# Layer 0's modulation rows over four column groups of TensorE, turned by a selector product

## The chip, the cores and the metric

One core of one Trainium2 chip runs the whole program. The metric is the device time of one execution in microseconds (us). The engines are TensorE (PE in the profile), VectorE (DVE), ScalarE (ACT), GpSimd (POOL) and SyncE (SP, which here only issues transfers). Each runs its own instruction list in order and they meet only at semaphores.

## The reference, cut to what matters

Two transformer blocks of two layers each run over 512 tokens of width 1024 (the first block carries 256 context tokens as well, 768 in all). At the head of each layer stands a modulation: a small matrix product of two conditioning vectors with a large weight.

```python
mod   = silu(c)     @ w_mod[l] + b_mod[l]     # for the 512 tokens
mod_c = silu(c_ctx) @ w_mod[l] + b_mod[l]     # for the 256 context tokens
sh1, sc1, ga1, sh2, sc2, ga2 = split(mod, 6)  # 1024 values each
h = rmsnorm(x, g_norm1[l]) * (1 + sc1) + sh1
pf, ... = split_proj(h @ w_in[l])             # pf: 256 Fourier features
y_f = fourier_mix(pf)
x = x + ga1 * (concat(y_f, y_m, y_a) @ w_out[l])
```

The change concerns layer 0 alone, and of it the first three of the six parts: shift (sh1), scale (sc1) and gate (ga1), 3072 values for each of two vectors. Everything is float32. Large products are made from values split in a high and a low part; the modulation's are plain float32 products.

## The kernel before

**Modulation tiles.** The weight of these 3072 columns comes as 12 tiles of 1 MB (`modw[0..11]`; 128 partitions, `KC` = 8 slices of 256 columns). They go through four slots (`MOD_FIRST`, each 2048 arena columns). `mod_row` (L799) works one tile: 8 products, each with a stationary operand of two columns (the two conditioning vectors' slice k, `cact`) and a moving operand of 256 columns, summed over k in PSUM on partitions 0 and 1. The profile shows two MATMUL records for each plain float32 product, so a tile is 16 records. Tiles 0 to 3 (shift) fill pair 0, tiles 4 to 7 (scale) pair 1, tiles 8 to 11 (gate) pair 2. A "pair" is two PSUM banks, 1024 columns.

**Turning.** ACT copies a pair's two rows to SBUF (`mod_rows`, L1588, into `rows_first`), and `turn(g)` (L807) makes eight PE transposes of 2 x 128 to bring the values onto partitions (into pair 3). DVE adds the bias there (`bias_added`).

**Order on PE.** `first_mod`: tiles 0 to 3, tiles 4 and 5, `turn(0)`, tiles 6 and 7. `norm`: column sums of squares for the rmsnorm (L780, L822), then `turn(1)`. `norm_mod` (L826): tiles 8 to 11. Then `fourier(768)`: `first_jobs` (L717), two feature jobs over 8 chunks k, 96 products in all, each chunk behind `h_wait(k)`, the signal that DVE has made `h_lo` chunk k. Then `pair_read(0)` and `pair_read(1)`, which wait until ACT has copied both jobs' results to `f_pf`; `turn(2)`; six jobs of the channel transform (L780), whose results DVE copies out in `values_read` (L2462); then the token transform (L929, L932) and the output projection (L712).

**Order on SP.** Conditioning vectors, tiles 0 to 3, x (3 MB), tiles 4 to 7, weight tile w0 into `raw[0]`, tiles 8 to 11, weight tile w1 into `raw[1]`, then `late_mod(12)` into `raw[0]` (a modulation tile that DVE folds, once w0 is split), `late_mod(13)` into `raw[1]` once w1 is split, and on. Each tile after the fourth waits until PE is done with the tile that last had its slot (`mod_used`).

**Order on ACT.** `mod_rows(0)`, eight squares of x, `mod_rows(1)`, the high part of w0 (`split`, L1551), the root of the norm (L1664, L1665), eight high parts of h (L1670), `mod_rows(2)`, the load of the Fourier constants, and in `fourier`: first the high part of w1 (`split`), then the two `f_pf` copies (L1741).

**Order on DVE.** The conditioning's silu, sums of squares, the low part of w0 (L2268), bias and gain, the chunks of h (L2483, L2490), and in `fourier`: the low part of w1, `late_fold(12)` (four long reductions, L2352), the gate's bias (after `turn(2)`), `values_read`, `late_fold(13)`.

Of the kernel before, what the change touches and what calls it, by code (L numbers as in the profile page):

```python
# [16 lines left out]
P = 128  # L17
# [85 lines left out]
def program(nc, io, per_pass):  # L103
    with ExitStack() as ctx:
# [3 lines left out]
        def sem(name):  # L108
            return ctx.enter_context(nc.semaphore(name))
# [114 lines left out]
        mod_folded = sem("mod_folded")  # L224
        rows_in = sem("mod_rows_in_sbuf")
        rows_turned = sem("mod_rows_turned")
        max_scores = sem("max_scores_ready")
        max_done = sem("max_reduced")
        maxt = sem("max_transposed")
# [18 lines left out]
        mod_first = [area(8 * T_ALL + i * KC * 256, KC, 256) for i in range(MOD_FIRST)]  # L248
        mod_ring = [area(12 * T_ALL + i * 2 * D, 2, D) for i in range(MOD_RING)]
        fold_products = area(4 * T_ALL, 2, D)  # L250
        rows_first = area(8 * T_ALL + MOD_FIRST * KC * 256, 1024, parts=2)

        n_sq = [area(i * T_ALL, T_ALL) for i in range(2)]
        n_acc = area(2 * T_ALL, T_ALL)
# [239 lines left out]
        def _(sp):  # L494
            t = Tally(sp, "sp", per_pass)
            def mod_tile(ti, slot):
                sp.dma_start(mod_first[slot].rearrange("p a b -> p (a b)"), io["modw"][ti]).then_inc(mod_in[slot], 16)

            sp.dma_start(small[:, 0:64], io["cv"]).then_inc(cv_in, 16)
            def mod_tiles(first, end):  # L500
                for ti in range(first, end):
                    if ti >= MOD_FIRST:

                        sp.wait_ge(mod_used, ti + 1)
                    mod_tile(ti, ti % MOD_FIRST)
            n_tiles = io["wt"].shape[0]

            def first_weights(*tiles):
# [20 lines left out]

            mod_tiles(0, MOD_FIRST)  # L530
            sp.dma_start(x[:].rearrange("p a b -> p (a b)"), io["xt"]).then_inc(x_in, 16)
            mod_tiles(MOD_FIRST, MOD_EARLY)
            first_weights(0)
            mod_tiles(MOD_EARLY, MOD_ROWS)
            first_weights(1)

            sp.wait_ge(w_lo_done, 0 + 3)
# [133 lines left out]
        def _(pe):  # L671
# [42 lines left out]
                                           stop=(k == kc - 1 and i == 2))  # L714
                mm.then_inc(signal, 1)

            def first_jobs(w, outs, n, signals):  # L717

                for k in range(KC):
                    h_wait(k)  # L720
                    for c, out in enumerate(outs):
                        for i, (a, b) in enumerate(passes(w, H)):
                            for lo, hi in segments(n):
                                mm = pe.matmul(out[:, lo:hi], a[:, k * 256 + c * P:k * 256 + (c + 1) * P], b[:, k, lo:hi],  # L724
                                               start=(k == 0 and i == 0), stop=(k == KC - 1 and i == 2))
                        if k == KC - 1:
                            mm.then_inc(signals[c], 1)
# [58 lines left out]
            def first_mod():  # L786

                pe.wait_ge(dve_pe, t.next(dve_pe))

                for ti in range(MOD_EARLY):  # L790
                    if ti % 4 == 0:
                        take_pair(ti // 4)
                    if ti == 6:

                        pe.wait_ge(const_in["start"], 32)
                        turn(0)
                    mod_row(ti, pp[ti // 4][0:2, ti % 4 * 256:(ti % 4 + 1) * 256])

            def mod_row(ti, out):  # L799

                slot = ti % MOD_FIRST
                pe.wait_ge(mod_in[slot], t.next(mod_in[slot], 16))
                for k in range(KC):
                    mm = pe.matmul(out, cact[:, 0, :, k], mod_first[slot][:, k, :], start=(k == 0), stop=(k == KC - 1))  # L804
                mm.then_inc(mod_used, 1)

            def turn(g):  # L807

                pe.wait_ge(rows_in, t.next(rows_in))
                for c in range(8):  # L810
                    at = S + 16 * g + 2 * c
                    mm = pe.transpose(pp[3][:, at:at + 2], rows_first[:, c * P:(c + 1) * P], ident[0:2, 0:2])
                mm.then_inc(rows_turned, 1)

            def norm(n):
# [7 lines left out]
                mm.then_inc(job_act, 1)  # L823
                turn(1)

            def norm_mod():  # L826

                take_pair(2)
                for ti in range(MOD_EARLY, MOD_ROWS):
                    mod_row(ti, pp[2][0:2, ti % 4 * 256:(ti % 4 + 1) * 256])  # L830

            def h_wait(k):

                pe.wait_ge(h_ready, t.next(h_ready))
# [67 lines left out]
            def fourier(n):  # L902
                w = tile()
                take_pair(0)
                take_pair(1)
                if n == S:
                    raw_first_jobs(w, (pp[0], pp[1]), S, False, tail_places(T_ALL), 2, (job_dve, tile_used))
                    t.next(h_ready, KC)
                else:
                    first_jobs(w, (pp[0], pp[1]), n, (job_act, tile_used))  # L910
                pair_read(0)
                pair_read(1)

                if n > S:
                    turn(2)
                pe.wait_ge(const_in["fourier"], t.next("fourier", 16))
                nt = n // P
                for i in range(nt):
                    tok = slice(i * P, (i + 1) * P)
                    plain_job(i % 2, [(pp[i % 2][:, c * 256:(c + 1) * 256], f_pf[:, c, tok], f_b, True, True)  # L920
                                      for c in range(2)], job_dve)
                pair_read(0)
                pair_read(1)
                for c in range(2):
                    cols = [slice(c * 256 + a * P, c * 256 + (a + 1) * P) for a in range(2)]
                    take_pair(c)
                    for a in range(2):
                        for i in range(NT):
                            mm = pe.matmul(pp[c][:, a * S:a * S + SH], f_v[:, i, cols[a]], f_c[:, a, i, :], start=(i == 0),  # L929
                                           stop=(i == NT - 1 and n == S), skip_group_check=True)  # L930
                        for i in range(2 if n > S else 0):
                            mm = pe.matmul(pp[c][:, a * S + SH:a * S + SH + CH], f_v[:, NT + i, cols[a]], f_cc[:, a, i, :],  # L932
                                           start=False, stop=(i == 1), skip_group_check=True)
                    mm.then_inc(job_act, 1)
                out_proj(2, P, n, 1, 8, 1024, fourier_wait)
# [568 lines left out]
            barrier()  # L1504
            first_mod()
            norm(T_ALL)
            norm_mod()
            for layer in range(2):
                n = T_ALL if layer == 0 else S
                fourier(n)  # L1510
# [14 lines left out]
        def _(act):  # L1525
# [48 lines left out]
            def first_mod():  # L1574
                act.dma_start(prm[:], io["prm"][0]).then_inc(const_in["prm"], 16)
                act.wait_ge(cv_in, 16)
                act.activation(cact[:], cvec, ACT.Exp, scale=-1.0).then_inc(act_dve, 1)

                act.wait_ge(cact_done, 1)
                for at in (0, 2):  # L1580
                    act.dma_start(io["crow"][at:at + 2].rearrange("v (p k) -> p v k", k=KC), cact[:, at])\
                       .then_inc(crow_out, 16)
                mod_rows(0, 0)
                for j in range(KC):
                    square(j, T_ALL)
                mod_rows(1, 1)

            def mod_rows(g, p):  # L1588

                act.wait_ge(mod_used, MOD_FIRST + 4 * (g + 1))  # L1590
                if g:
                    act.wait_ge(rows_turned, g)
                finish(act.activation(rows_first, pp[p][0:2, :], ACT.Copy), pair_free[p], rows_in)

            def spread_conditioning(slot, row):
                act.dma_start(crow[:, slot, :], io["crow"][row:row + 1].to_broadcast([P, D])).then_inc(crow_in, 16)

            def late_rows():
                mod_rows(2, 2)
                fourier_constants()  # L1600

            def square(j, n):

# [132 lines left out]
            def fourier(n):  # L1736
                if n > S:
                    split()
                for c in range(2 if n > S else 0):
                    job(last=c == 1)  # L1740
                    act.activation(f_pf[:, c, 0:n], pp[c][:, 0:n], ACT.Copy).then_inc(pair_free[c], 1)  # L1741
                k = SH + CH if n > S else SH
                for c in range(2):
                    job()
                    act.activation(f_s[:, c, 0:k], pp[c][:, S:S + k], ACT.Copy).then_inc(act_dve, 1)

                    act.wait_ge(dve_act, t.next(dve_act))
                    act.activation(u_hi[:, c, 0:n], f_y[:, c, 0:n], ACT.Copy).then_inc(act_dve, 1)
                split()
# [458 lines left out]
            act.dma_start(gfin[:], io["gfin"]).then_inc(const_in["start"], 16)  # L2208
            barrier()
            first_mod()  # L2210
            split()
            norm(T_ALL, 0)
            late_rows()
            for layer in range(2):
                n = T_ALL if layer == 0 else S
                if layer:
# [19 lines left out]
        def _(dve):  # L2236
# [143 lines left out]
            def first_mod():  # L2380
                heard()
                finish(dve.tensor_scalar(cact[:], cact[:], 1.0, None, ALU.add))
                finish(dve.reciprocal(cact[:], cact[:]))
                finish(dve.tensor_tensor(cact[:], cact[:], cvec, ALU.mult), dve_pe, cact_done)

                dve.wait_ge(x_in, 16)
                dve.sem_inc(x_done, KC)
                for j in range(KC):
                    add_square(j, T_ALL)
                for s in range(MOD_RING):  # L2390
                    t.next(mod_in[s], 16 * (MOD_ROWS // MOD_FIRST))
                split()

                dve.wait_ge(const_in["prm"], t.next("prm", 16))
# [1039 lines left out]
```

## Time and profile before

| | us |
|---|---|
| median of 3 runs | 3429.74 |
| lowest, highest | 3429.38, 3435.35 |
| profiled execution, first to last instruction | 3431.3 |
| PE busy in it | 3316.9 (97%) |
| from the start to the first product of the token transform (L929) | 82.20 |

The page gives one execution; its span is 1.6 us above the median of the timed runs. PE is busy in nearly all of it. The stage that the change touches is the first 82 us. A timeline row gives its start and length in us, the engine, the line, the operation, the output and inputs, and the number of instructions merged; in brackets stands the idle time before it and what ended it. SPq and ACTq rows are transfers being issued, not the transfers themselves.

### The profile page before, as it was taken

The numbers are of one execution on the slowest core, as the hardware profiler recorded it, in microseconds if no ns is written. First come the engines' busy times: TensorE is split into PE (matmuls) and PEld (weight loads), VectorE is DVE, ScalarE is ACT, GpSimd is POOL, SyncE is SP. The second block draws the span as 40 slices with busy tenths as digits, with TensorE's granted clock in tenths as the row PEclk, the third lists the DMA queues.
The fourth block names the chain that finished last, engine by engine and source line by source line (L and its number), as shares of the span: only waits on it lengthen the run. The fifth ranks groups of instructions, "written<-read, shape, count | busy, mean of one in ns | idle before, by whom it ended". The sixth has DMA issues, their size and how long they took to land.

```text
span 3431.3 us, 42870 instructions
## 1 busy us (share of the span) xinstructions
PE 3316.9 (97%) x16496; PEld 2652.5 (77%) x16496; DVE 2051.2 (60%) x2561; ACT 1248.9 (36%) x1564; POOL 337.2 (10%) x328
## 2 busy tenths in 40 slices
PE   8999989999999998999998999999999999999999
PEld 4777768888887776688885677788887577878887
DVE  4676777555466566565567755465557766364443
ACT  3245353221223454532234533242225433343222
POOL 0000011100111000111121100011112011001000
PEclk9999999999999999999999999999999999999999
DMA  6331123323222222154432122244443132222223
GB/s 277 112 108 59 60 81 123 112 98 130 102 98 76 78 79 79 42 198 171 171 133 70 54 68 84 98 150 178 165 168 107 36 99 71 92 102 92 93 97 110
DMA packets 61594, 370.59 MB, mean 108 GB/s; under 512 B 9416, under 2 KB 10056, under 8 KB 20368
## 3 DMA queue, kind: packets, MB, share of 16 engines
q1 hardware_dynamic: 45120, 275.31, 22.9%
q10 hardware_dynamic: 16336, 93.39, 7.3%
q8 instruction: 93, 1.52, 0.2%
q14 instruction: 45, 0.37, 0.0%
HBM read 354.27 MB, written 2.33 MB: 104 GB/s over the span
## 4 chain that ended last, share of the span: by engine, by line
PE 80%; DVE 12%; ACT 5%; issue 3%; DMA 1%; POOL 0%; DVEq 0%; ACTq 0%; SPq 0%; POOLq 0%
PE pair L712 50%; PE pair L1185 8%; PE pair L863 6%; PE pair L750 2%; PE pair L780 2%; DVE w_lo L2268 2%; PE pair L1018 1%; PE pair L1254 1%; PE pair L724 1%; ACT w_hi L1551 1%; PE pair L804 1%; PE pair L1080 1%; DVE mxg L2862 1%; PE pair L1237 1%; PE pair L1388 1%
## 5 line engine op out<-in xcount | busy, mean ns | idle before, releaser
L2268 DVE TENSOR_TENSOR w_lo<-raw,w_hi 128x2048 fp32r<-128x2048 f32 x221 | 509.8, 2307 | 284.1 <-ACT w_hi L1551 279.1
L1551 ACT ACTIVATE w_hi<-raw 128x2048 fp32r<-128x2048 f32 x221 | 421.6, 1908 | 619.6 <-PE pair L712 523.2
L712 PE MATMUL pair<-h_hi,w_hi 128*128 128x512 f32 (+2 forms) x1856 | 595.5, 363 | 5.7 <-DVEq L2250 2.7
L712 PE MATMUL pair<-h_lo,w_hi 128*128 128x512 f32 (+2 forms) x1856 | 594.5, 362 | 0.0
L712 PE MATMUL pair<-h_hi,w_lo 128*128 128x512 f32 (+2 forms) x1856 | 594.3, 362 | 0.0
L712 PE MATMUL pair<-u_hi,w_hi 128*128 128x512 f32 x1116 | 373.3, 370 | 12.2 <-DVEq L2260 4.9
L712 PE MATMUL pair<-u_hi,w_lo 128*128 128x512 f32 x1116 | 370.8, 367 | 0.0
L712 PE MATMUL pair<-u_lo,w_hi 128*128 128x512 f32 x1116 | 370.7, 367 | 0.0
L2531 DVE TENSOR_TENSOR u_lo<-arena,u_hi 128x512 fp32r<-128x512 f32 (+1 forms) x128 | 97.2, 759 | 447.3 <-POOL arena L3099 447.0
L712 PEld LDWEIGHTS pair<-h_hi,w_hi 128*128 128x128 f32 (+2 forms) x1856 | 309.4, 183 | 67.7 <-issue 7.3
L712 PEld LDWEIGHTS pair<-h_hi,w_lo 128*128 128x128 f32 (+2 forms) x1856 | 309.5, 183 | 61.2
L712 PEld LDWEIGHTS pair<-h_lo,w_hi 128*128 128x128 f32 (+2 forms) x1856 | 309.4, 183 | 60.4
L2309 DVE SCALAR_TENSOR_TENSOR x<-pair,mod,x 128x512 f32<-128x512 f32 x336 | 223.5, 690 | 162.4 <-PE pair L712 148.8
L3099 POOL TENSOR_TENSOR arena<-arena 128x512 f32<-128x512 f32 (+1 forms) x128 | 172.1, 1345 | 1339.5 <-ACT u_hi L1702 1247.2
L1701 ACT ACTIVATE arena<-pair 128x512 f32<-128x512 f32 (+1 forms) x120 | 78.2, 652 | 462.9 <-PE pair L712 462.8
L712 PEld LDWEIGHTS pair<-u_hi,w_hi 128*128 128x128 f32 x1116 | 193.9, 189 | 50.9 <-issue 7.6
L1185 PE MATMUL pair<-h_hi,w_hi 128*128 128x512 f32 x544 | 226.8, 417 | 1.8 <-DVE w_lo L2268 1.5
L2365 DVE CUSTOM_DVE_ANT_0 arena<-arena,crow 128x1024 f32<-128x1024 f32 x192 | 225.1, 1219 | 0.0
L712 PEld LDWEIGHTS pair<-u_lo,w_hi 128*128 128x128 f32 x1116 | 194.0, 189 | 34.8 <-issue 0.2
L712 PEld LDWEIGHTS pair<-u_hi,w_lo 128*128 128x128 f32 x1116 | 193.6, 189 | 35.0
L1185 PE MATMUL pair<-h_lo,w_hi 128*128 128x512 f32 x544 | 215.9, 397 | 0.0
L1185 PE MATMUL pair<-h_hi,w_lo 128*128 128x512 f32 x544 | 215.3, 396 | 0.0
(377 smaller groups left out, 4888.6 us busy)
## 6 DMA issues: line engine op xcount, KB each, us to landing
raw<-in_wt_dram SPq DMA_DIRECT2D x222, 1024.0 KB, 4.8
arena<-in_modw_dram ACTq DMA_DIRECT2D x72, 1024.0 KB, 5.0
arena<-in_modw_dram SPq DMA_DIRECT2D x12, 1024.0 KB, 8.7
raw<-in_modw_dram SPq DMA_DIRECT2D x12, 1024.0 KB, 4.7
arena<-arena SPq DMA_DIRECT2D x136, 64.0 KB, 2.0
arena<-negm_rows_dram ACTq DMA_DIRECT2D x16, 384.0 KB, 4.3
x<-in_xt_dram SPq DMA_DIRECT2D x1, 3072.0 KB, 18.6
arena<-in_fconst_dram ACTq DMA_DIRECT2D x2, 1414.0 KB, 6.1
```

Source lines behind the costliest of these rows:

```text
L712: mm = pe.matmul(pp[p][0:m, lo:hi], a[0:rows, k * width + c0:k * width + c0 + m], b[0:rows, k, lo:hi], start=(k == 0 and i == 0), stop=(k ...
L750: mm = pe.matmul(out[:, lo:hi], a[:, k * 256 + c * P:k * 256 + (c + 1) * P], v, start=first, stop=(k == KC - 1 and i == 2 and (not spread ...
L780: mm = pe.matmul(out, a, b, start=first, stop=last)
L863: mm = pe.matmul(pp[c + 1][:, lo:hi], a[:, k * 512 + c * P:k * 512 + (c + 1) * P], b[:, k, lo:hi], start=(k == 0 and i == 0), stop=(k == 3 ...
L1185: mm = pe.matmul(bank(slot), a[:, k * width + c0:k * width + c0 + P], b[:, k, 0:S], start=(k == 0 and i == 0), stop=(k == KC - 1 and i == 2))
L1551: act.activation(w_hi[slot][:], raw[slot][:], ACT.Copy).then_inc(w_hi_done, 1)
L1701: finish(act.activation(m_r[c][:, 0:n], pp[p][:, 0:n], ACT.Relu), pair_free[p])
L2268: dve.tensor_tensor(w_lo[slot][:], raw[slot][:], w_hi[slot][:].bitcast(F32), ALU.subtract)\
L2309: ins = dve.scalar_tensor_tensor(x[:, j, a:b], pp[p][:, a:b], mod[:, 16 + 24 * which + j, s:s + 1], x[:, j, a:b], ALU.mult, ALU.add)
L2365: ins = dve.tensor_tensor_reduce(out=w if v == vectors - 1 else fold_products[:, a, :], in0=w, in1=crow[:, v, :], scale=1.0, scalar=0.0, o ...
L2531: dve.tensor_tensor(u_lo[:, 2 * half + c, 0:n], m_f[c][:, 0:n], U32[:, 2 * half + c, 0:n], ALU.subtract).then_inc(hid_lo, 1)
L3099: pool.tensor_tensor(m_f[i % 2][:, 0:n], m_r[i % 2][:, 0:n], m_r[i % 2][:, 0:n], ALU.mult)\
```

## The change

Each modulation product now writes 32 partitions. The stationary operand is 32 columns wide (`cond_rows`: 16 copies of each of the two vectors), and slices k = 2g and 2g + 1 go to output partitions 32g to 32g + 31, in two rounds over g = 0 to 3. So a pair holds four partial sums, of two slices each. `cond_rows` lies in `raw[1]`, the place of weight tile w1. ACT copies all 128 partitions instead of two. `turn` makes eight plain float32 products of a 128 x 128 stationary slice of `rows_first` with a moving operand of two columns, `row_sel`, which has a one at partitions 32g (or 32g + 16) and adds the four partial sums while it turns them.

The four gate tiles leave `norm_mod`: two are worked before chunk 5 of `first_jobs`, two after its end. All four use slots 2 and 3. w0 is loaded ahead of tiles 6 and 7; w1 is loaded only after PE is done with tile 11. ACT splits w0 before `mod_rows(1)`, issues the load of the Fourier constants right after `mod_rows(1)`, and does `mod_rows(2)` after the `f_pf` copies.

```diff
@@ SP
-                        sp.wait_ge(mod_used, ti + 1)
-                    mod_tile(ti, ti % MOD_FIRST)
+                        sp.wait_ge(mod_used, ti + 1 if ti < MOD_EARLY else ti + 3)
+                    mod_tile(ti, mod_slot(ti))
...
-            mod_tiles(MOD_FIRST, MOD_EARLY)
+            mod_tiles(MOD_FIRST, 6)
             first_weights(0)
+            mod_tiles(6, MOD_EARLY)
             mod_tiles(MOD_EARLY, MOD_ROWS)
+
+            sp.wait_ge(mod_used, MOD_FIRST + MOD_ROWS)
             first_weights(1)
@@ PE
+                    if k == 5 and between:
+                        between()
                     h_wait(k)
...
-                for k in range(KC):
-                    mm = pe.matmul(out, cact[:, 0, :, k], mod_first[slot][:, k, :], start=(k == 0), stop=(k == KC - 1))
+                for half in range(2):
+                    for g in range(4):
+                        k = 2 * g + half
+                        mm = pe.matmul(out[32 * g:32 * g + 32], cond_rows[:, k, :],
+                                       mod_first[slot][:, k, :], start=(half == 0), stop=(half == 1))
...
-                    mm = pe.transpose(pp[3][:, at:at + 2], rows_first[:, c * P:(c + 1) * P], ident[0:2, 0:2])
+                    mm = pe.matmul(pp[3][:, at:at + 2], rows_first[:, c * P:(c + 1) * P], row_sel, start=True, stop=True)
...
-                    first_jobs(w, (pp[0], pp[1]), n, (job_act, tile_used))
+                    first_jobs(w, (pp[0], pp[1]), n, (job_act, tile_used), lambda: gate_mod(MOD_EARLY))
+                    gate_mod(MOD_EARLY + 2)
...
-            norm_mod()
@@ ACT
+                split()
                 mod_rows(1, 1)
+                fourier_constants()
...
-                finish(act.activation(rows_first, pp[p][0:2, :], ACT.Copy), pair_free[p], rows_in)
+                finish(act.activation(rows_first, pp[p][:], ACT.Copy), pair_free[p], rows_in)
...
+                if n > S:
+                    mod_rows(2, 2)
...
-            split()
             norm(T_ALL, 0)
-            late_rows()
@@ DVE
-                finish(dve.tensor_tensor(cact[:], cact[:], cvec, ALU.mult), dve_pe, cact_done)
+                finish(dve.tensor_tensor(cact[:], cact[:], cvec, ALU.mult), cact_done)
+                finish(dve.tensor_copy(cond_rows.rearrange("p k (v r) -> p k v r", r=16),
+                                       cact[:, 0].rearrange("p v k -> p k v").unsqueeze(3).to_broadcast([P, KC, 2, 16])),
+                       dve_pe)
+
+                dve.wait_ge(const_in["start"], 32)
+                finish(dve.tensor_reduce(row_sel, ident[:].rearrange("p (j w) -> p w j", w=32)[:, 0:32:16, :], AX.X, ALU.add),
+                       sel_ready)
```

## Rows read from the trace of the kernel before

**Rows 1.** The page: span, and busy time of each engine.

```profile
span 3431.3 us, 42870 instructions
...
PE 3316.9 (97%) x16496; PEld 2652.5 (77%) x16496; DVE 2051.2 (60%) x2561; ACT 1248.9 (36%) x1564; POOL 337.2 (10%) x328
```

**Rows 2.** Chain of waits, first 135 us: start, length, what.

```profile
13.50 11.27 DMA arena<-in_modw_dram
...
42.91 13.91 PE pair L804 x64
56.82 17.15 PE pair L724 x96
...
75.54 5.84 PE pair L780 x24
...
81.41 0.70 DVE arena L2462
```

**Rows 3.** Timeline of SP's issues, first 50 us.

```profile
28.55 11.36 SPq L497 DMA_DIRECT2D arena<-in_modw_dram  x4
39.96 0.43 SPq L512 DMA_DIRECT2D raw<-in_wt_dram  x1
```

**Rows 4.** Stretches: busy us by engine, then granted clock, DMA share, GB/s.

```profile
25.00:28.50 3.50, 3.50 (x17) 1.35 (x16) 2.17 (x3) 3.07 (x4) 0.00 (x0) 1.00 1.01 426
```

**Rows 5.** Timelines from 7 and from 42 us: the modulation products.

```profile
7.15 6.10 PE L804 MATMUL pair<-arena,cact 128*2 128x256 f32 x15 [7.15 <-DMA arena<-in_modw_dram]
...
42.84 13.98 PE L804 MATMUL pair<-arena,cact 128*2 128x256 f32 x64
```

**Rows 6.** Timeline of PE: grouped-query scores, two 64-row halves of the array.

```profile
1844.21 0.39 PE L1224 MATMUL pair<-u_hi 64*128 64x512 f32 x2
1844.44 0.39 PE L1224 MATMUL pair<-u_hi,u_lo 64*128 64x512 f32 x2
```

**Rows 7.** Timeline of PE: products with four and two moving columns.

```profile
3080.13 0.25 PE L733 MATMUL pair<-shift,w_hi 128*128 128x4 f32 x1
3080.24 0.25 PE L735 MATMUL pair<-shift,w_lo 128*128 128x2 f32 x1
```

**Rows 8.** Timeline, 42 to 48 us: turning, the norm's root, first chunks.

```profile
42.26 0.65 PE L812 MATMUL pair<-ident,arena 2*128 2x2 f32 x8
...
43.67 0.84 ACT L1665 ACTIVATE arena<-arena 128x768 f32<-128x768 f32 x1
...
45.00 0.18 DVE L2403 TENSOR_TENSOR mod<-pair,prm 128x32 f32<-128x32 f32 x1
...
45.43 2.21 DVE L2483 SCALAR_TENSOR_TENSOR arena<-x,gain,arena 128x512 f32<-128x512 f32 x4
...
47.77 1.15 DVE L2490 SCALAR_TENSOR_TENSOR h_lo<-arena,mod,h_hi 128x512 fp32r<-128x512 f32 x2
```

**Rows 9.** Stretches around an idle TensorE; columns as in Rows 4.

```profile
90.80:93.10 2.30, 0.38 (x4) 0.18 (x2) 1.15 (x4) 0.51 (x2) 0.00 (x0) 1.00 0.02 7
...
94.90:97.90 3.00, 2.93 (x9) 2.54 (x10) 2.16 (x2) 0.83 (x1) 0.00 (x0) 0.50 0.00 0
```

**Rows 10.** Timeline, 61 to 83 us, ACT and DVE: what follows w1's arrival.

```profile
61.63 1.00 ACT L1593 ACTIVATE arena<-pair 2x1024 f32<-2x1024 f32 x1
...
63.25 1.92 ACT L1551 ACTIVATE w_hi<-raw 128x2048 fp32r<-128x2048 f32 x1 [0.62 <-ACT arena L1593]
65.20 2.29 DVE L2268 TENSOR_TENSOR w_lo<-raw,w_hi 128x2048 fp32r<-128x2048 f32 x1 [2.30 <-ACT w_hi L1551]
...
72.11 0.08 DVE L2352 DVE_READ_ACCUMULATOR2_ANT mod_sum<- 128x1 f32 x1
...
74.01 0.81 ACT L1741 ACTIVATE arena<-pair 128x768 f32<-128x768 f32 x1 [0.25 <-PE pair L724]
...
76.71 1.48 DVE L2462 COPY arena<-pair 128x512 f32<-128x512 f32 x2 [0.96 <-PE pair L780]
```

**Rows 11.** Transfers issued from 60 to 80 us: size, median us to landing.

```profile
raw<-in_wt_dram SPq DMA_DIRECT2D x1, 1024.0 KB, 4.7
```

More of the change, by code:

```diff
@@ L226, in program @@
         rows_turned = sem("mod_rows_turned")
+        sel_ready = sem("row_selector_ready")
         max_scores = sem("max_scores_ready")
@@ L250, in program, with mod_slot @@
         fold_products = area(4 * T_ALL, 2, D)
-        rows_first = area(8 * T_ALL + MOD_FIRST * KC * 256, 1024, parts=2)
+        rows_first = area(8 * T_ALL + MOD_FIRST * KC * 256, 1024)
+        row_sel = small[:, 74:76]
+        cond_rows = raw[1][:, 0:KC * 32].rearrange("p (k w) -> p k w", w=32)
+        def mod_slot(ti):
+            return ti % MOD_FIRST if ti < MOD_EARLY else 2 + ti % 2
         n_sq = [area(i * T_ALL, T_ALL) for i in range(2)]
@@ L715, in feature_job, with first_jobs @@
                 mm.then_inc(signal, 1)
-            def first_jobs(w, outs, n, signals):
+            def first_jobs(w, outs, n, signals, between=None):
                 for k in range(KC):
+                    if k == 5 and between:
+                        between()
                     h_wait(k)
@@ L793, in first_mod @@
                     if ti == 6:
-                        pe.wait_ge(const_in["start"], 32)
+                        pe.wait_ge(sel_ready, 1)
                         turn(0)
-                    mod_row(ti, pp[ti // 4][0:2, ti % 4 * 256:(ti % 4 + 1) * 256])
+                    mod_row(ti, pp[ti // 4][:, ti % 4 * 256:(ti % 4 + 1) * 256])
             def mod_row(ti, out):
-                slot = ti % MOD_FIRST
+                slot = mod_slot(ti)
                 pe.wait_ge(mod_in[slot], t.next(mod_in[slot], 16))
-                for k in range(KC):
-                    mm = pe.matmul(out, cact[:, 0, :, k], mod_first[slot][:, k, :], start=(k == 0), stop=(k == KC - 1))
+                for half in range(2):
[3 more added lines that the diff above has]
+                                       mod_first[slot][:, k, :], start=(half == 0), stop=(half == 1))
                 mm.then_inc(mod_used, 1)
@@ L824, in norm, with gate_mod @@
                 turn(1)
[L826 to L830, printed above, removed]
+            def gate_mod(first):
+                if first == MOD_EARLY:
+                    take_pair(2)
+                for ti in range(first, first + 2):
+                    mod_row(ti, pp[2][:, ti % 4 * 256:(ti % 4 + 1) * 256])
             def h_wait(k):
@@ L1592, in mod_rows @@
                     act.wait_ge(rows_turned, g)
-                finish(act.activation(rows_first, pp[p][0:2, :], ACT.Copy), pair_free[p], rows_in)
+                finish(act.activation(rows_first, pp[p][:], ACT.Copy), pair_free[p], rows_in)
             def spread_conditioning(slot, row):
                 act.dma_start(crow[:, slot, :], io["crow"][row:row + 1].to_broadcast([P, D])).then_inc(crow_in, 16)
-            def late_rows():
-                mod_rows(2, 2)
-                fourier_constants()
             def square(j, n):
@@ L2390, in first_mod @@
                 for s in range(MOD_RING):
-                    t.next(mod_in[s], 16 * (MOD_ROWS // MOD_FIRST))
+                    t.next(mod_in[s], 16 * sum(mod_slot(ti) == s for ti in range(MOD_ROWS)))
                 split()
```

## The prediction

> **What bounds the kernel now.** I read the page first: PE is busy 3317 of 3431 us [rows 1]. What delays PE anywhere shifts all behind it, as each engine works its list in order and no later stretch is slack for PE, so the question is when PE reaches a point behind the change. I take the start of the token transform (L929), 82.20 before.
>
> Then the chain of waits [rows 2]. Tile 4 of the modulation arrives at 24.77, and PE is the chain nearly throughout from there: tiles 4 to 7 and the norm until 42.91, the four gate tiles (13.91 us), the 96 products of the Fourier jobs (17.15 us), six channel jobs (5.84 us), a last copy. Behind the chain stands memory: between 25 and 28.5 us the transfers fill their engines at 426 GB/s [rows 4], so 1 MB lands every 2.46 us. SP's list [rows 3] shows when PE is done with slots: the last issue of the four starts 0.43 us before 39.91, at 39.5, and that is the end of tile 7.
>
> **Tiles 4 to 7.** A tile is 16 records of 0.218 us (13.98 / 64), 3.5 us; the first ones, from 7.15, came 0.41 us apart (6.10 / 15), the half level of the clock, though the granted clock is written as full there [rows 5]. How fast the new products go no row shows. Bounds: no overlap, 3.5 us a tile; full overlap of four groups, 0.87 us. The nearest rows are the attention scores over two row halves of the array: a pair of products with 512 columns starts every 0.23 us [rows 6], while one product over the full array averages 0.24 us for 512 columns (96 products of 512 or 256 columns in 17.15 us [rows 2]). So independent parts of the array do work at the same time when neighbours in the list use different ones. In the new list the neighbours are different groups only every other time: a float32 product is two records, and both use the same group. If PE starts products in order, the second record of group 0 waits for the first, group 1's first starts with it, and so on: eight steps of 0.218 us, 1.75 us a tile. I take that.
>
> The Trainium skill ("TensorE: Matmul & The Clock Gate", Part 3) says that packed products start about 4 ns apart, which would make a tile 0.87 us; it also says that products start and end in program order, from which the halving follows. No row here has column groups. The skill's "TensorEngine Tiling (Array Packing)", Tiling Modes, adds that a change of mode drains the engine; with some twelve changes that speaks against the change, by an amount that no row shows.
>
> The order of landing becomes tile 4 at 24.8, tile 5 27.2, w0 29.7, tile 6 32.2, tile 7 34.6, since w0 goes ahead of two tiles. PE now waits for memory: tile 7 ends at 34.6 + 0.1 + 1.75 = 36.5, against 39.5. Of the 7 us that the products of four tiles save, 4 go to the wait for memory.
>
> **Norm and turn(1).** From 39.5 to 42.91 is 3.4 us, of which the eight transposes are 0.65 [rows 8], so the norm is 2.8. The turn becomes 16 records, each with 128 stationary columns. Products with four and two moving columns start 0.11 us apart [rows 7], so 1.8 us (bounds 0.65, were they as cheap as transposes, and 3.6 at the half clock). Turn(1) ends at 36.5 + 2.8 + 1.8 = 41.1. The norm's root ended at 44.51, 5.0 after tile 7 [rows 8], now 41.5. Before, DVE began the bias only at 45.00, after the low part of w0; that is now earlier and gone from the path. First chunk product: 41.1 + 0.1 + 0.43 = 41.6, against 45.43. The first chunk of h is done 3.5 us later (48.92 before), at 45.1.
>
> **The Fourier jobs.** Before, PE began them at 56.82, with the gate tiles as cover for DVE's chunks. Now it begins at 45.1 after 4 us of idleness. After a stretch with 0.38 of 2.3 us busy, the granted clock was 0.50 for 3 us [rows 9]. I add 1.7 us, half of some 3.4. Chunks come every 2.1 us (DVE: two products and two low parts of 0.55 and 0.57 us each [rows 8]), PE needs 17.15 / 8 = 2.1, so PE doesn't catch up. The gate tiles add 4 x 1.75 = 7.0. Tiles 10 and 11 are loaded when 8 and 9 are done, some 8 us before PE wants them. PE is done with tile 11 at X = 45.1 + 17.15 + 1.7 + 7.0 = 71.0, against 73.97 for the jobs before. So far a gain of 3.0.
>
> **w1, the step that decides.** Before, w1 was asked for at 39.96 [rows 3] and split at 63.25, beside PE's jobs. `cond_rows` now lies in `raw[1]`, so SP asks for w1 only at X. Queued behind that wait are late tiles 12 and 13 and w2. And ACT's list has the split of w1 ahead of the two `f_pf` copies, for which PE waits in `pair_read`. From X:
> - w1 lands at +4.7 [rows 11], ACT starts at +4.85 and ends at +6.8 (1.92 [rows 10]).
> - ACT: copies 2 x 0.81, `mod_rows(2)` 1.0, to +9.5. PE: turn(2) to +11.3, then two channel jobs to +13.3; it needs a pair back for the third.
> - DVE: low part of w1 to +9.1 (2.29). Tile 12, asked for right behind w1, landed at +7.3. Fold to +13.8 (from 67.5 to 72.2 before, 4.7 [rows 10]), hidden then behind the jobs and exposed now, since the fold stands ahead of `values_read` in DVE's list. Bias, first copy: +14.8 (0.69).
> - Four channel jobs of 0.97, last copy 0.7, reactions 0.2: L929 at +19.6. PE idled 9.5 us before, so its clock is low again; much of that hides behind DVE, and I add 0.8 (bounds 0 and 4).
>
> L929 starts at 71.0 + 20.4 = 91.4, 9.2 us later than 82.20. Behind it the lists are as before: fold 13 follows `values_read`, w2 is asked for at +13.8 and needed over 10 us later. So the 9.2 us stay.
>
> **What is free.** DVE's copy into `cond_rows` and the sum for `row_sel`: DVE has nothing else before x lands, and PE waits for tile 0 until 7.15 [rows 5]; were tile 0 earlier, some 0.4 us. ACT's copy of 128 partitions in place of two: same columns, 1.0 us. The constants and two spreads are issued by ACT while PE does the norm. Were they 0.6 us slower, they would delay the root.
>
> **Rivals.**
> A, the forecast: two-fold overlap and w1's load on the path, +9.2, 62%. Own range +8 to +15 (half clock in tiles 6 and 7, the norm, the turns and the channel jobs).
> B, full overlap: each tile 0.87 us. Tile 7 ends 0.9 earlier, the gate tiles save 3.5 more; X = 66.6, L929 87.0, +4.8, 3434.5 us. That is not slower as far as can be told. For it: rows 6, where a pair costs as one. Against: the two records of one group stand next to each other. It decides from the point where a tile falls under some 1.2 us, as the loss is then under 6.9. 22%. (The page on TensorE of the Trainium skill, Part 3, states this case's mechanism.)
> C, no overlap: a tile stays at 3.5. Tile 7 ends at 24.9 + 14.0 + 1.8 (turn) + 1.7 (clock) = 42.4, X = 83.8, L929 104.2, +22, 3451.8. For it: wide float32 operands were never seen in parallel here. 12%.
> D, faster: w1's split is hidden after all (it would have to be off ACT's list before the copies, which the code denies), with full overlap and a clock that stays up. Then the channel jobs start at X + 1.1 + 1.8, that is 66.6 + 2.9 - 1.7 = 67.8, against 75.54: -7.7, 3422.0. With the two-fold overlap and a falling clock it is only -1.6. 4%. That the change doesn't do what it says (groups not used at all) is C.
>
> **How the numbers follow.** The sum is made against the profiled execution, 3431.3 + 9.2 = 3440.5; the timed median is 1.6 lower, so 3438.9. 0.2% is 6.9 us, about what a measurement of this kernel can tell from no change. The range takes in B less 1 us and A with every clock penalty: 3433.5 to 3446; C and D, 16%, stay out. Slower: A nearly whole and C, 72%. Same: B and the low edge of A, 24%. Faster: D, 4%.
>
> **What would show it.** A tile's eight products in 1.75 us at full clock, tile 7 done by 36.5 and h's first chunk at 45; the start of w1's transfer at the end of tile 11, ACT waiting for it and PE idle for 9 us; fold 12 ahead of the first copy of `values_read`; L929 at 91. Wrong would make it: a tile of 0.9 or 3.5 us; a copy of `f_pf` ahead of w1's split; a stretch behind L929 that takes up the delay.

## The result

| | before | changed |
|---|---|---|
| timed runs, median | 3431.39 us (12 runs) | 3439.33 us (12 runs) |
| ratio to before | 1 | 1.0019 (95% interval 1.0012 to 1.0026) |
| end of tile 7 | 39.5 | 37.1 |
| first Fourier jobs start | 56.8 | 46.0 |
| all modulation tiles and first jobs done | 74.0 | 69.4 |
| token transform starts | 82.2 | 90.3 |

The change makes the kernel slower, by 1.9 in a thousand, 6.5 us (4.1 to 8.9); the two medians lie 7.9 us apart. The forecast was 9.2 us at the start of the token transform; there the profile shows 8.1 (90.27 against 82.20).

The chain of waits of the changed kernel, first 140 us (start, length, what), goes through the decisive stretch. The line numbers have moved: L817 is the modulation products (L804 before), L735 the first jobs (L724), L791 the channel jobs (L780), L826 the turns, L945 the token transform (L929).

```profile
16.92 18.22 DMA arena<-in_modw_dram
35.15 0.04 issue
35.19 1.93 PE pair L817 x16
...
45.99 13.04 PE pair L735 x60
59.03 1.86 PE pair L817 x32
60.90 6.56 PE pair L735 x36
67.45 1.91 PE pair L817 x32
69.36 0.02 issue
69.38 4.70 DMA raw<-in_wt_dram
...
75.91 1.49 ACT arena L1754 x2
77.41 0.92 ACT arena L1610
...
78.58 3.55 PE pair L826 x16
82.13 7.33 PE pair L791 x24
89.46 0.02 issue
89.48 0.70 DVE arena L2482
...
90.27 1.98 PE pair L945 x8
```

Where [rows 2] had PE nearly alone from 42.91 on, two transfers stand in the chain now. The first is the wait for tile 7, which lands at 35.15. The second begins when PE is done with tile 11, at 69.36: w1 is asked for at 69.38 and lands 4.70 later. Two rows of the timeline show what stood behind it on ACT, where [rows 10] had the split at 63.25 beside PE's jobs.

```profile
74.10 1.91 ACT L1566 ACTIVATE w_hi<-raw 128x2048 fp32r<-128x2048 f32 x1 [15.45 <-DMA raw<-in_wt_dram]
...
75.91 1.49 ACT L1754 ACTIVATE arena<-pair 128x768 f32<-128x768 f32 x2
```

ACT sat idle 15.45 us for w1, and the two `f_pf` copies came only after its split, at 75.91, although the jobs had ended at 67.45. DVE had a chain of its own behind w1: its low part and then fold 12, whose last row stands here with the first copy of `values_read`:

```profile
82.95 0.08 DVE L2365 DVE_READ_ACCUMULATOR2_ANT mod_sum<- 128x1 f32 x1
...
84.15 0.69 DVE L2482 COPY arena<-pair 128x512 f32<-128x512 f32 x1 [0.79 <-PE pair L791]
```

DVE waited 0.79 us for PE's first channel job, so in this kernel the chain over ACT and PE ended last, by that little. PE stood still from 69.4 to 78.6, and its clock had fallen when it went on. The stretches show that (busy us of PE, PEld, DVE, ACT and POOL, each with its instructions, then granted clock, DMA share, GB/s; cf. [rows 9]):

```profile
44.00:51.00 7.00, 5.01 (x15) 4.30 (x16) 6.87 (x14) 3.97 (x8) 0.00 (x0) 0.53 0.62 217
51.00:59.00 8.00, 8.00 (x50) 6.85 (x50) 7.87 (x16) 4.50 (x8) 0.00 (x0) 0.99 0.01 2
69.50:78.40 8.90, 0.00 (x0) 0.00 (x0) 2.36 (x2) 4.22 (x4) 0.00 (x0) 0.62 0.60 236
78.60:85.50 6.90, 6.90 (x25) 6.25 (x26) 5.26 (x10) 0.00 (x0) 0.00 (x0) 0.51 0.63 209
```

The turn and the first two channel jobs ran at the half level (0.51), and so did the first chunks of the jobs after the idle time before them (0.53).

The span of this one profiled execution is 3431.0 us, no longer than the 3431.3 of before. The 8 us had not gone at first: the low part of one weight tile starts at 1318.71 against 1311.21, still 7.5 late. Some 5 us of it were made up around 1900, where in the profiled execution of before the clock was low once more and in this one it was not. From the start of one low part on DVE to the start of another, the same 324 products took 74.42 us before and 69.29 us in the changed kernel:

```profile
1848.08:1922.50 74.42, 68.85 (x324) 40.21 (x322) 56.17 (x65) 34.45 (x48) 1.28 (x1) 0.91 0.12 40
```

```profile
1855.82:1925.11 69.29, 63.11 (x324) 37.22 (x322) 56.07 (x65) 34.38 (x48) 1.28 (x1) 1.00 0.13 43
```

Whether that is chance I can't say. The same stretch took 69.3 to 70.1 us in the profiles of all five kernels that work the gate tiles among and after the first jobs (changed, rows elsewhere, copies first, moves alone, a group's slices in a row), 74.5 in that of late w1 in the kernel of before, and 71.5 to 74.5 in those of the other four.

Single executions of one kernel lie some 10 us apart (3427.8 to 3435.8 us before, 3432.2 to 3443.7 after), so I judge a stage by the start of the token transform in its profile, and a version by the ratio of its timed runs.

### The profile page after: what moved, and what is told of

The parts are those of the page before. It is cut to its first block, busy times and chain, and to the rows that moved or that the text cites. A ratio compares the mean times of both kernels' runs of the same rounds, so it can differ in the third digit from the quotient of the medians.

```text
span 3431.0 us, 42940 instructions
## 1 busy us (share of the span) xinstructions
PE 3294.4 (96%) x16520; PEld 2648.4 (77%) x16520; DVE 2050.4 (60%) x2563; ACT 1249.1 (36%) x1564; POOL 340.8 (10%) x328
## 4 chain that ended last, share of the span: by engine, by line
PE 80%; DVE 10%; ACT 5%; issue 3%; DMA 1%; POOL 0%; DVEq 0%; ACTq 0%; SPq 0%; POOLq 0%
PE pair L721 50%; PE pair L1201 9%; PE pair L878 6%; PE pair L761 2%; PE pair L791 2%; DVE w_lo L2281 2%; PE pair L1034 1%; PE pair L1270 1%; PE pair L735 1%; PE pair L1121 1%; ACT w_hi L1566 1%; DMA arena<-in_modw_dram 1%; PE pair L1096 1%; DVE mxg L2882 1%; PE pair L1404 1%
```

## The experiments

The landmarks of all of them, in us from the start of the profile:

| kernel | tile 7 done | jobs start | tile 11 and jobs done | token transform | ratio to before |
|---|---|---|---|---|---|
| before | 39.5 | 56.8 | 74.0 | 82.2 | 1 |
| changed | 37.1 | 46.0 | 69.4 | 90.3 | 1.0019 (1.0012 to 1.0026) |
| rows elsewhere | 37.0 | 47.6 | 70.2 | 81.7 | 0.9998 (0.9988 to 1.0007) |
| copies first | 37.3 | 47.9 | 70.5 | 91.8 | one run |
| moves alone | 39.8 | 48.2 | 81.4 | 102.9 | one run |
| late w1 in the kernel of before | 39.1 | 56.4 | 73.5 | 81.8 | one run |
| a group's slices in a row | 37.2 | 45.9 | 69.2 | 90.1 | one run |
| groups alone | 36.5 | 48.0 | 66.4 | 78.9 | 0.9982 (0.9972 to 0.9991) |
| both | 37.3 | 46.9 | 67.6 | 77.6 | 0.9976 (0.9966 to 0.9986) |
| split first | 36.5 | 46.2 | 63.4 | 76.3 | 0.9979 (0.9970 to 0.9988) |
| constants early | 34.5 | 46.1 | 63.3 | 74.4 | 0.9970 (0.9957 to 0.9982) |

A landmark of one profile moves by a us or two without any change in the lists: copies first has the list of the changed kernel up to the end of tile 11, and its jobs start 1.9 us later, as its norm began at the half level (2.93 us for the first four sums, against 1.79).

### Is it w1's load? The spread conditioning in a place of its own

```diff
+        cond_sb = sb("cond_sb", [P, KC * 32])
-        cond_rows = raw[1][:, 0:KC * 32].rearrange("p (k w) -> p k w", w=32)
+        cond_rows = cond_sb[:].rearrange("p (k w) -> p k w", w=32)
...
-            mod_tiles(MOD_EARLY, MOD_ROWS)
-
-            sp.wait_ge(mod_used, MOD_FIRST + MOD_ROWS)
             first_weights(1)
+            mod_tiles(MOD_EARLY, MOD_ROWS)
```

> The changed kernel with one thing undone: the spread conditioning (cond_rows) has 1 KB per partition of its own instead of raw[1], so w1 is asked for right behind tile 7. Theory 1 (the prediction's): w1's load from the end of tile 11, with ACT's split, DVE's low part and fold 12 behind it, is the loss. Then ACT splits w1 at about 60, PE is still done with tile 11 at 69.4, turn(2) ends at 72.2, fold 12 (tile 12 asked for at 62, landing at 69) ends at 73.8, and the token transform starts at 79.5 instead of 90.3: 10.8 us less than the changed kernel, 2.7 less than before, ratio to before 0.999. Theory 2: the loss comes from the low clock of PE around its waits, and w1 merely fills a time that would be lost anyway: the token transform starts at 86 or later, and the time stays within 3 us of the changed kernel's.

The token transform starts at 81.7, 8.6 us earlier than in the changed kernel, though PE was 0.8 later at the end of tile 11; the ratio is 0.9998. Theory 1 holds. Most of what was left over of the expected 10.8 is the next item in the same queue, late tile 12, which made fold 12 end at 75.8 where 73.8 was expected. PE (first row) and DVE (second and third) in the timeline:

```profile
71.59 1.92 PE L825 MATMUL pair<-small,arena 128*128 128x2 f32 x16 [1.35 <-ACTq L1557]
```

```profile
71.04 1.23 DVE L2364 CUSTOM_DVE_ANT_0 arena<-raw,crow 128x1024 bf16<-128x1024 f32 x1 [6.71 <-DMA raw<-in_modw_dram]
...
76.20 1.29 DVE L2481 COPY arena<-pair 128x512 f32<-128x512 f32 x2
```

PE turns 7 us earlier than in the changed kernel, at the full clock. DVE then waits 6.71 us for tile 12, which SP asks for at 62.25, behind tiles 10 and 11, and folds it ahead of the copies.

### Is it ACT's order? The copies ahead of w1's split

```diff
-                if n > S:
-                    split()
                 for c in range(2 if n > S else 0):
-                    job(last=c == 1)
+                    job(last=c == 1, ahead=-1)
...
                 if n > S:
                     mod_rows(2, 2)
+                    split()
```

> The changed kernel, w1 still loaded after tile 11, but ACT makes the two f_pf copies and copies the gate rows ahead of the split of w1. Theory 1a: behind w1 there are two chains, ACT's to PE and DVE's (low part of w1, fold 12, then values_read), and DVE's is nearly as long. Then PE turns at 70.6 to 72.4 and makes two channel jobs by 74.4, but waits for values_read until 84; the token transform starts at 88.5, only 1.8 us earlier. Theory 1b: only ACT's order holds PE, and DVE's work fits beside it: the token transform starts at 79.2.

PE turned at 71.81, right after its own work as expected, and had two channel jobs done at 75.6. Then it stood 9.74 us:

```profile
73.59 1.97 PE L791 MATMUL pair<-arena 128*128 128x256 f32 x8
85.30 5.70 PE L791 MATMUL pair<-arena 128*128 128x256 f32 x16 [9.74 <-DVE arena L2481]
```

The token transform starts at 91.8, 21.3 us after the end of tile 11, against 20.9 in the changed kernel. Theory 1a holds, and more than I had given it: the 1.8 us expected did not come, since the new wait lowers the clock for the remaining jobs (5.70 us for four). Two chains of nearly the same length follow w1, one over ACT to PE and one over DVE (low part, fold 12, `values_read`). Shortening only the one over ACT gained nothing.

### The moves with the products of before

```diff
-                for half in range(2):
-                    for g in range(4):
-                        k = 2 * g + half
-                        mm = pe.matmul(out[32 * g:32 * g + 32], cond_rows[:, k, :],
-                                       mod_first[slot][:, k, :], start=(half == 0), stop=(half == 1))
+                for k in range(KC):
+                    mm = pe.matmul(out[0:2], cact[:, 0, :, k], mod_first[slot][:, k, :], start=(k == 0), stop=(k == KC - 1))
...
-                    mm = pe.matmul(pp[3][:, at:at + 2], rows_first[:, c * P:(c + 1) * P], row_sel, start=True, stop=True)
+                    mm = pe.transpose(pp[3][:, at:at + 2], rows_first[0:2, c * P:(c + 1) * P], ident[0:2, 0:2])
```

> The changed kernel's order of work (gate tiles among the jobs, w1 behind tile 11) with the products and the turns of before: two stationary columns, eight products in a row, transposes. Theory 1 (late w1 costs about 20 us from the end of tile 11 to the token transform, whatever the products are): tile 7 ends at 39.5 as before, the first jobs start at 48, PE is done with tile 11 at 81.8 and the token transform starts at 101.6, 19 us later than before. Rival (the column groups bring a cost of their own, in the turns or in changes of mode, that is hidden in the 21 us): the distance from the end of tile 11 to the token transform is under 17 us.

The end of tile 11 came at 81.4 and the token transform at 102.9, 21.5 us later. So the 21 us between the two belong to the order of work and not to the column groups; this kernel took 3448.65 us in its one run. The groups and the cheap transposes are exchanged here with little effect on that distance (20.9 in the changed kernel), which is what two chains of nearly one length mean. Here DVE's chain ended last: PE had two channel jobs done and waited 0.90 us for the first copy. The distance from tile 11 was under-sized in my expectation by 1.7 us, as the last four channel jobs took 5.90 us, where they take 3.91 at the full clock with the rows elsewhere:

```profile
96.22 5.89 PE L791 MATMUL pair<-arena 128*128 128x256 f32 x16 [0.90 <-DVE arena L2479]
```

### Late w1 in the kernel of before

```diff
             mod_tiles(MOD_EARLY, MOD_ROWS)
+
+            sp.wait_ge(mod_used, MOD_FIRST + MOD_ROWS)
             first_weights(1)
```

> The kernel of before with one line added: w1 is asked for only when all twelve modulation tiles are worked. Theory 1: the late request is harmless where the gate tiles stand ahead of the jobs. They are done at 56.8, w1 lands at 61.6, ACT splits it at 63.3 as before, and the token transform starts at 82.2, with no difference. Rival: the request is dear by itself, as late tile 12 and what follows on SP shift by 17 us; then fold 12 starts after 67.4 and the token transform moves by 1 us or more.

w1 was asked for at 56.41 and ACT split it at 62.81. The stretch from the start of the first jobs to the token transform took 25.4 us, as before (81.76 - 56.38; 82.20 - 56.82). In this one run the request for w1 behind all modulation tiles cost nothing by itself. It costs when the last modulation tiles stand behind the jobs, whose 17 us had covered it.

### How the column groups overlap

```diff
-                for half in range(2):
-                    for g in range(4):
+                for g in range(4):
+                    for half in range(2):
```

> The changed kernel with the loops of a modulation tile swapped: both slices of a column group one after the other (four records in a row for the same group) before the next group. It measures how products of different groups overlap. In the changed kernel a tile took 0.97 us at the full clock. If PE starts products strictly in order, each group's first record can start no sooner than the last of the group before, so 13 steps of 0.22 us, 2.8 us for a tile at the full clock, and 5.6 at the half one. If each group has its work ahead of it and runs by itself, 0.97 and 1.93 as before.

A tile took 1.96 us at the half level and two took 1.97 at the full one, as against 1.93 and 1.93 for the order of the change:

```profile
58.83 1.97 PE L817 MATMUL pair<-arena,raw 128*32 128x256 f32 x32
67.17 1.97 PE L817 MATMUL pair<-arena,raw 128*32 128x256 f32 x32
```

So the order of groups in the list hardly matters, even with four records of one group in a row. In-order starts would have made it 2.8 us a tile at the full clock. The records of both kernels start in bursts of four, a burst every 0.22 us. These are the first burst of a tile in the changed kernel and in this one:

```profile
58.96 0.42 PE L817 MATMUL pair<-arena,raw 128*32 128x256 f32 x4
```

```profile
58.83 0.44 PE L817 MATMUL pair<-arena,raw 128*32 128x256 f32 x4
```

A record doesn't name its group. But records of one group came 0.22 us apart before the change, so the four of a burst are, as I read it, one of each group, also where the list has four of one group in a row.

### The column groups alone, in the order of before

```diff
-            return ti % MOD_FIRST if ti < MOD_EARLY else 2 + ti % 2
+            return ti % MOD_FIRST
...
-            mod_tiles(MOD_FIRST, 6)
+            mod_tiles(MOD_FIRST, MOD_EARLY)
             first_weights(0)
-            mod_tiles(6, MOD_EARLY)
             mod_tiles(MOD_EARLY, MOD_ROWS)
-
-            sp.wait_ge(mod_used, MOD_FIRST + MOD_ROWS)
             first_weights(1)
...
             norm(T_ALL)
+            gate_mod(MOD_EARLY)
+            gate_mod(MOD_EARLY + 2)
```

> The order of before with the column groups and the selector product alone; cond_rows has its own 1 KB, so nothing waits for w1. Theory 1: the products are a gain by themselves. Tile 7 ends at 36, the four gate tiles are done by 46, while DVE makes h's first chunks, and keep PE's clock up; jobs end at 63.2, DVE's fold 12 then ends at 70, and the token transform starts at 75.7: 6.5 us less than before, ratio 0.998. Theory 2 (cold products and dearer turns eat the gain): the token transform starts at 80 or later, ratio 0.9995 or more.

`cond_rows` has its own place here too, and ACT's order is that of before. The ratio is 0.9982 (0.9972 to 0.9991), 6 us faster than before; the profile shows 3.3 us at the token transform (78.9). Theory 1 holds in its sign and is off in its size by 3 us. One row says where the first two went:

```profile
46.91 1.07 PE L815 MATMUL pair<-arena,cond_sb 128*32 128x256 f32 x16 [2.68 <-DMA arena<-in_modw_dram]
```

The last gate tile lands at 46.9, as memory serves the conditioning rows (1 MB on ACT's queue) at the same time, so the jobs start at 48.0. The jobs lost most of the rest, 18.37 us for 17.15, with their first chunks at the half level. Behind them the 12.5 us that I had expected came true for another reason: turn(2) took 2.6 us and the channel jobs 8.2 instead of 5.8, for the clock had fallen (0.50 from 70 to 74), while fold 12 ended at 69.1, ahead of the turn's end at 69.9, so DVE held nothing up.

### Both ways together

```diff
@@ against the kernel with the groups alone
-            gate_mod(MOD_EARLY + 2)
...
-                    first_jobs(w, (pp[0], pp[1]), n, (job_act, tile_used))
+                    first_jobs(w, (pp[0], pp[1]), n, (job_act, tile_used), lambda: gate_mod(MOD_EARLY + 2))
...
-                act.wait_ge(crow_out, 32)
-                spread_conditioning(0, 0)
-                spread_conditioning(1, 1)
                 job()
...
             norm(T_ALL, 0)
+            act.wait_ge(crow_out, 32)
+            spread_conditioning(0, 0)
+            spread_conditioning(1, 1)
             mod_rows(2, 2)
```

> A version meant to beat both: the column groups and the selector product, cond_rows in its own 1 KB, slots in turn as before the change, w0 loaded after tile 7 and w1 after tile 11 without a wait, two gate tiles ahead of the first jobs and two ahead of chunk 5, the Fourier constants and the spread of the conditioning rows issued after h. Theory 1: tile 7 lands at 32.4, PE is done with it at 34.3, h's first chunk at 43.4, PE done with all first jobs at 62.5, the token transform starts at 72 instead of 82.2: 10 us less than before, ratio 0.997. Theory 2 (low clock): the idle time between tiles stays, jobs and turns at the half clock cost 4 to 6 us, the token transform starts at 77 or later, ratio 0.9985 or more.

The ratio is 0.9976 (0.9966 to 0.9986), the token transform starts at 77.6. Theory 2 was right about the stage, where its landmark was "77 or later", and wrong about the ratio, where it had 0.9985 or more. All tiles before the norm ran at the half level (1.82 to 1.94 each, turn(0) 3.50), which the granted clock shows here (0.53; the last three numbers are clock, DMA share and GB/s):

```profile
20.00:37.00 17.00, 10.64 (x80) 6.15 (x80) 6.31 (x7) 6.64 (x8) 0.00 (x0) 0.53 1.00 417
```

In this execution the first tile had landed at 8.4, 1.1 later than in the changed kernel's. And fold 12 began only at 66.95, as ACT had the copy of the gate rows (after tile 11, 61.1) ahead of w1's split at 62.8; that is the order that the next kernel turns round. The timed gain, 8 us, lies above the stage's 4.6 but its interval (4.8 to 11.7) begins close to it; I don't count the difference as found.

### w1's split first, then the constants early

```diff
@@ against the kernel with the groups alone
             norm(T_ALL, 0)
+            split()
             mod_rows(2, 2)
...
-                if n > S:
-                    split()
                 for c in range(2 if n > S else 0):
...
                 for j in range(KC):
+                    if j == 2:
+                        act.wait_ge(crow_out, 32)
+                        spread_conditioning(0, 0)
+                        spread_conditioning(1, 1)
```

> As the run with the groups alone, with w1's split ahead of the copy of the gate rows on ACT and the spread of the conditioning rows issued after the second chunk of h, so that fold 12 is done before values_read. Theory 1: the last wait before the token transform is then PE's own list: jobs end at 63.2, turn(2) at 66.8, six channel jobs, the token transform at 73.5, 2 us less than with the groups alone and 8.7 less than before, ratio 0.9975. Rival: w1 or the spread rows land too late for the fold (after 68), and nothing is won over the groups alone.

Fold 12 ends at 67.4, in time, and the token transform starts at 76.3, 2.6 us earlier than with the groups alone; the ratio, 0.9979, can't be told from that kernel's. The jobs end at 63.4 as expected. The next to come last was a load that had not mattered before, the Fourier constants, asked for at 61.5:

```profile
68.02 1.22 PE L789 MATMUL pair<-arena 128*128 128x256 f32 x2 [1.77 <-DMA arena<-in_fconst_dram]
```

In the last kernel they are asked for after the third chunk of h:

```diff
+                    if j == 3:
+                        act.wait_ge(mod_used, MOD_FIRST + MOD_ROWS)
+                        fourier_constants()
...
             mod_rows(2, 2)
-            fourier_constants()
```

> As the run with w1's split first, with the Fourier constants asked for after the third chunk of h (all gate tiles are done by then) instead of behind the copy of the gate rows. In the run before, PE stood 1.8 us for them, at 66.2, and its clock fell. Theory 1: the channel jobs start at 66.3 and, at the full clock, take 5.9 us, so the token transform starts at 73.1, 3 us earlier than in that run and 9 us earlier than before the change; ratio to before 0.997. Theory 2 (the clock falls anyway, through the 0.95 us wait for the copies and the turn): the channel jobs take 7.4 us again and the token transform starts at 74.5.

```profile
64.25 1.92 PE L824 MATMUL pair<-small,arena 128*128 128x2 f32 x16 [0.95 <-issue]
66.03 7.49 PE L789 MATMUL pair<-arena 128*128 128x256 f32 x24
74.35 1.98 PE L942 MATMUL pair<-arena 128*128 128x257 f32 x8 [0.83 <-DVE arena L2482]
```

By the chain of waits the channel jobs start at 66.2 and still take 7.4 us: theory 2. The clock falls there without the wait for the constants (0.54 from 66 to 68). The token transform starts at 74.4, 7.9 us earlier than before the change, and the ratio is 0.9970 (0.9957 to 0.9982), 10 us faster than before and, by the two ratios, some 17 faster than the changed kernel. This version beats both.

## Why the prediction was right, and where not

**The bound and w1.** Right, step by step: tile 7 waits for memory (35.15 landed, 34.6 forecast), PE idles before the jobs (4.2 us), w1 is asked for at the end of tile 11, ACT waits for it with the `f_pf` copies behind it, PE stands 9.2 us. From the end of tile 11 to the token transform it was 20.9 us for 20.4. Three runs show that this is the loss: without the late load 8.6 us of it go; with the products of before it is 21.5; and where the gate tiles stand ahead of the jobs a late w1 costs nothing. Two chains of nearly equal length stand there, as the sum had them, but it had DVE's fold as the later one, by 1.5 us (+14.8 for +13.3), and in the changed kernel PE came last, by 0.79, with a cold turn of 3.55 us for 1.8.

**The products.** Wrong in mechanism: I let the second record of a group hold back the next group and got 1.75 us a tile. At the full clock a tile takes 0.97 (two in 1.93), so all four groups run at once, as rival B had it. The change into and out of the groups, whose price no row had shown, costs about 0.1 us each time: the first jobs' pairs of products start 0.35 us apart, and 0.44 or 0.45 apart where two tiles begin or have just ended. The Trainium skill ("TensorE: Matmul & The Clock Gate", Part 3) gives a packed set one product's time plus some ns, which this comes near: four records of 0.218 are 0.87. Its strict order of starts, from which I had drawn the halving, didn't show between groups: four records in a row for one group changed a tile by 0.03 us.

**The clock.** Mis-sized. Tiles 6 and 7 ran at the half level, 1.93 each, which by chance lies near the 1.75 that I took for the full one, so the end of tile 7 (37.1 for 36.5) looked right. The gate tiles ran at the full clock and took 3.8 us for 7.0. The jobs, after their idle time, lost 2.5 us for 1.7 (13.04 + 6.56 against 17.15). The 3.4 us of which I took half stand in no row: [rows 9] show 3.0 at the half level, and the jobs ran there for 5.2, from 45.99 to about 51.2. The turn with two columns took 1.69 at the full clock (1.8 forecast) and 3.55 at the half one. So tile 11 ended at 69.4 for 71.0: 3.2 us too dear in the gate tiles, 0.9 too cheap up to the start of the jobs (46.0 for 45.1) and 0.8 too cheap in the clock of the jobs.

**The rivals.** B had the right product time and put the token transform at 87.0; it came at 90.3. Of the 3.3 us the half clock took 1.0 at tile 7 and 0.8 in the jobs, tile 7's later landing 0.5, the tail 0.5, small terms the rest. C is out by the tile times. Against D the order in ACT's list held: the split stands ahead of the copies. And D's condition was not enough: with the copies ahead of the split DVE's chain held PE, and the transform started at 91.8. With the load off the path, full overlap and a clock that fell, the gain was 0.5 us at the token transform, where D had 1.6 with the two-fold overlap.

**The size.** 9.2 us forecast, 8.1 at the landmark, 6.5 (4.1 to 8.9) in the timed ratio. That it came so near is partly luck: tile 11 was 1.6 us early, as the tiles that were forecast too dear outweighed a clock forecast too cheap, and the tail made up 0.5 of that. The median, 3439.33 for 3438.9, is nearer still because the median of before over twelve runs lies 1.7 us above the three that the forecast went by. The range's upper end is not its own sum either: +15 gives 3444.7, not 3446.

That the delay stays behind the token transform isn't shown. In the one profile of the changed kernel it is still 7.7 us at 1770 and then mostly goes, with the granted clock; in the timed runs 6.5 us of it are there. The profiles of all five kernels with the gate tiles among and after the first jobs gain 4 to 5 us on that of before at the same place, so a part that is given back regularly is not ruled out.

## What to carry to other kernels

Before a buffer is lent to a new use, follow the load that has to wait for its return, and everything that stands behind that load in each engine's list: here 4.7 us of transfer became 9 us of idle PE, because copies of finished results stood behind a split on ACT and, on DVE, a fold hung on the same load. Turning round only the one list moved the idle time and didn't shorten it. Before work is moved, ask what it had covered; here the gate tiles had covered the making of h, with PE at the full clock, and the jobs behind them had covered w1. And when a faster product ends in a wait, price what follows at the half clock.

## What the runs showed of the hardware

- Products on four groups of 32 columns of the array run at the same time: eight float32 products of 128x256 take 0.97 us at the full clock and 1.93 at the half one, against 3.5 us for the eight with two columns in one group, in both orders of the groups that were tried.
- Faster products can spend more of their time at the half level. Before the change PE was busy without a break from 7.15 to 23.8, records came 0.22 us apart from about 13.5 on, and after a wait of 1.1 us for tile 4 still did. With the groups it waits 0.3 to 0.7 us for the landing of most tiles and 8 us for tile 4, and in the changed kernel's profile every tile up to 37 took 1.93 or 1.94 us, twice the 0.97 of the gate tiles. (The granted clock column of the changed kernel reads 1.00 in that stretch; that of the kernel "both" reads 0.53 with nearly the same tile times, which is why I go by the times.) The short waits alone don't keep the clock down: with the rows elsewhere tile 3 ran at the full level behind them, and tile 4, after 8.8 us of waiting, at the half one again. So it was in the profiles of copies first and the groups alone.

```profile
14.83 1.07 PE L816 MATMUL pair<-arena,cond_sb 128*32 128x256 f32 x16 [0.88 <-DMA arena<-in_modw_dram]
24.72 1.94 PE L816 MATMUL pair<-arena,cond_sb 128*32 128x256 f32 x16 [8.82 <-DMA arena<-in_modw_dram]
```

- The six channel jobs took 5.8 us before and 7.4 us in the kernels "split first" and "constants early", after 17 us of dense jobs, some 1 us of waiting and a turn of 1.9 us with two moving columns (in "split first" also 1.8 us for the constants); with the rows elsewhere, behind a wait of 1.35 us and the same turn, and in "both", behind 0.95 us and the same turn, they ran at the full clock. What decides was not tried.
